# One program block for the state space stage of a hybrid trunk layer: set-up, four turns and end part written out, with one run of gate columns

## The reference

```python
def ssm_mixer(u, lam_re, lam_im, log_dt, b_re, b_im, c_re, c_im, d_skip, glu_w, glu_b):
    ...
    _, _, xr, xi = lax.associative_scan(combine, (a_r, a_i, bur, bui), axis=1)
    y = (jnp.einsum('bsgp,gcp->bsgc', xr, c_re.astype(f32))
         - jnp.einsum('bsgp,gcp->bsgc', xi, c_im.astype(f32))).reshape(B, S, SSM_WIDTH)
    y = jax.nn.gelu(y + d_skip.astype(f32) * uf)
    y = y * jax.nn.sigmoid(y @ glu_w.astype(f32) + glu_b.astype(f32))
    return y.astype(u.dtype)
...
        ga, gb, gc = jnp.split(jax.nn.sigmoid(h @ gate_w[l] + gate_b[l]), N_BRANCHES, axis=-1)
```

## Time and profile before

| | us |
|---|---|
| median of 3 runs | 3227.89 (3226.14 to 3228.81) |
| the profiled execution | 3229.56 |
| its span, first to last instruction | 3227.3 |
| TensorE busy in it | 2858.8 (89%) |
| VectorE busy | 1984.2 (61%) |
| ScalarE busy | 1472.7 (46%) |
| GpSimd busy | 390.5 (12%) |

### The profile page before, as it was taken

How to read it: one execution, slowest core, us unless ns; L and a number is a source line. 1 busy time by engine, 2 the same in 40 slices (tenths; PEclk the granted TensorE clock), 3 DMA queues, 4 the chain that set the end, 5 groups by cost and what they waited for, 6 DMA issues and landing times. The chain is left out here.

```text
span 3227.3 us, 41692 instructions
## 1 busy us (share of the span) xinstructions
PE 2858.8 (89%) x13494; PEld 2213.1 (69%) x13495; DVE 1984.2 (61%) x3048; ACT 1472.7 (46%) x2363; POOL 390.5 (12%) x296
## 2 busy tenths in 40 slices
PE   4999998999999987889995987994899999999994
PEld 3767666676767765777774776883677777777772
DVE  6657994545454554544353654225788888888883
ACT  4315553545555552222233332121566666666662
POOL 3101220000000001110010000110122122222211
PEclk9999998999999998888897998996999999999997
DMA  6374324141313136211117996542889997866864
GB/s 234 103 244 169 96 92 144 33 134 37 121 44 115 40 115 203 66 43 45 42 62 270 291 298 215 178 159 111 310 282 298 348 355 248 279 213 215 282 191 137
DMA packets 289051, 553.55 MB, mean 172 GB/s; under 512 B 30745, under 2 KB 97561, under 8 KB 284834
## 3 DMA queue, kind: packets, MB, share of 16 engines
q1 hardware_dynamic: 271010, 500.45, 44.8%
q0 software_dynamic: 14112, 51.39, 6.7%
q10 hardware_dynamic: 3808, 0.14, 0.1%
HBM read 417.16 MB, written 143.15 MB: 174 GB/s over the span
## 5 line engine op out<-in xcount | busy, mean ns | idle before, releaser
L2512 DVE TENSOR_TENSOR moe_w_lo<-moe_W,moe_w_hi 128x1024 fp32r<-128x1024 f32 x392 | 471.3, 1221 | 84.4 <-ACT moe_w_hi L2448 80.1
L2448 ACT CAST moe_w_hi<-moe_W 128x1024 fp32r (+1 forms) x392 | 409.2, 1050 | 145.8 <-PE moe_h1b L2379 77.6
L1573 PE MATMUL project_bank<-h_lo,w_hi 128*128 128x512 f32 x512 | 204.6, 400 | 0.0
L515 DVE TENSOR_SCALAR_CACHE_REDUCE att_S<-att_bank 128x512 f32<-128x512 f32 x192 | 125.0, 689 | 120.3 <-PE att_bank L303 120.3
L336 PE MATMUL att_bank<-h_hi,w_hi 128*128 128x512 f32 x384 | 171.1, 445 | 14.1 <-PEq L137 10.8
L2404 PE MATMUL moe_yb<-moe_W,moe_hT 128*128 x384 | 172.8, 593 | 0.0
L2377 PE MATMUL moe_h1b<-moe_w_hi,moe_xT_hi 128*128 128x512 f32 x384 | 157.1, 409 | 3.8 <-DVE moe_xT_lo L2523 3.8
L421 ACT ACTIVATE att_S<-att_S,att_nm 128x128 f32<-128x128 f32 (+15 forms) x128 | 154.1, 1206 | 0.0
L337 PE MATMUL att_bank<-h_lo,w_hi 128*128 128x512 f32 x384 | 153.0, 398 | 0.0
L2378 PE MATMUL moe_h1b<-moe_w_lo,moe_xT_hi 128*128 128x512 f32 x384 | 152.6, 397 | 0.0
L338 PE MATMUL att_bank<-h_hi,w_lo 128*128 128x512 f32 x384 | 152.6, 397 | 0.0
(11 more groups left out here) (460 smaller groups left out, 6980.3 us busy)
## 6 DMA issues: line engine op xcount, KB each, us to landing
moe_W<-in_moe_w SPq DMA_DIRECT2D x96, 2048.0 KB, 10.6
w_raw<-in_gate_w SPq DMA_DIRECT2D x48, 512.0 KB, 3.7
out_sg<-gateT SPq DMA_DIRECT2D x32, 768.0 KB, 8.3
gateT<-att_gates SPq DMA_DIRECT2D x48, 256.0 KB, 2.4
gateT<-gate_out SPq DMA_DIRECT2D x48, 256.0 KB, 2.4
early<-in_ada_w SPq DMA_DIRECT2D x8, 1024.0 KB, 9.6
project_spare<-in_x SPq DMA_DIRECT2D x16, 512.0 KB, 6.8
w_raw<-in_w_in SPq DMA_DIRECT2D x16, 512.0 KB, 4.2
```

Source lines behind the costliest of these rows:

```text
L1573: pe.matmul(bank[n % 4][:], w_hi[b][:, k, :], low[:, k, at512(tb)], start=False, stop=False)
L2448: nc.scalar.copy(w_hi[:, slot(p, first), :], raw(at, p)).then_inc(q["w13_high"], 1)
L2512: nc.vector.tensor_tensor(w_lo[:, own, :], raw(at, p), w_hi[:, own, :].bitcast(F32), ALU.subtract).then_inc(q["w1_low" if p < 4 else "w3_l ...
```

## The change

Set-up, turns and end part become one block. The loop is written out in the Python source (`for tn in range(TURNS)`), so each turn has its own instructions and its indices are constants. The five `s.end()` between the parts are gone (the one at the stage's end stays); semaphores run on through the turns, their values counted up with `tn`. One `GateFill` of 21 chunks takes the place of the three kinds of run, so that `higher` of a part's first chunk stands behind the last `out` of the part before. The bias is read from `gate_bias` at a constant column, and GpSimd's copy of it (`take_bias`) goes. The copies to `ucp` and `c1` for a turn are made in the turn ahead of it, behind its last RJ. VectorE builds E of a turn before it waits for the y products of the turn ahead (`y_summed`), and `apt` and M2 behind that wait. A semaphore `set_up` tells ScalarE and VectorE that C2 is there.

The diff, cut to its core:

```diff
-            "gb": gate_bias,
-            "gbt": sb("gate_gbt", [P, 8], ctx=ctx)}
+            "gb": gate_bias}
...
-    def take_bias(self, pool):
-        self.nc.gpsimd.tensor_copy(self.tiles["gbt"][:, :self.count], self.tiles["gb"][:, bass.ds(self.c0, self.count)]).then_inc(self.biased, 1)
...
-        if u == 0:
-            act.wait_ge(self.biased, 1)
-                                  bias=self.tiles["gbt"][:, u // 2:u // 2 + 1]).then_inc(self.placed, 1)
+                                  bias=self.tiles["gb"][:, self.c0 + u // 2:self.c0 + u // 2 + 1]).then_inc(self.placed, 1)
...
-        fill_set = GateFill(nc, g, s, tiles, h_hi, h_lo, 3, 4, 0)
+        fill = GateFill(nc, g, s, tiles, h_hi, h_lo, 3, 21, 0, last=True)
...
+                for tn in range(TURNS):
+                    for u in range(8 + 6 * tn, 14 + 6 * tn):
+                        fill.store(sp, u)
...
+                for j in range(20):
+                    fill.lower(pool, j)
...
+                pe.wait_ge(q["placed"], 8)
                 for n in range(KD, 8 * KD):
-                    fill_set.group(pe, n)
+                    fill.group(pe, n)
+
+                for tn in range(TURNS):
+                    ident = const(g, "ident")
+                    base = (8 + 6 * tn) * KD
+                    pe.wait_ge(q["u_copied"], 2 * tn + 1)
+                    for b in range(2):
+                        for gi in (2 * b, 2 * b + 1):
+                            for f in range(2):
+                                at = (gi % 2) * SC + f * P
+                                mm = pe.transpose(bank[b][:, at:at + P], ucp[:, f, gi, :], ident)
+                        mm.then_inc(q["u_turned"], 1)
+                    for done in range(8):
+                        fill.group(pe, base + done)
...
+                    pe.wait_ge(q["u_copied"], 2 * tn + 2)
...
+                    pe.wait_ge(q["m_placed"], tn + 1)
+                    if tn:
+                        pe.wait_ge(q["y_placed"], 2 * tn)
+                    for b in range(2):
...
+                for tn in range(TURNS):
+                    mine = slice(tn * GU, (tn + 1) * GU)
+                    if tn == 0:
+                        act.wait_ge(q["placed"], 8)
+                        nc.scalar.copy(ucp[:], UY[:, :, mine, :]).then_inc(q["u_copied"], 1)
+                        act.wait_ge(q["set_up"], 1)
+                        nc.scalar.copy(c1[:], C1[:, mine, :]).then_inc(q["u_copied"], 1)
+                    for b in range(2):
+                        act.wait_ge(q["u_turned"], 2 * tn + b + 1)
+                        nc.scalar.copy(U[:, 2 * b:2 * b + 2, :].rearrange("p g n -> p (g n)"), bank[b][:]).then_inc(q["u_placed"], 1)
+                    fill.out(act, 8 + 6 * tn)
+                    act.wait_ge(q["m2_ready"], tn + 1)
+                    for lv in range(LEVELS):
+                        if lv in (2, 4, 6):
+                            fill.out(act, 8 + 6 * tn + lv // 2)
+                        for gi in range(GU):
+                            if LEVELS * tn + lv >= 2:
+                                act.wait_ge(q["r_ready"], GU * (LEVELS * tn + lv - 2) + gi + 1)
+                            nc.scalar.activation(RJ[:, lv % 2, gi, :], const(g, "swap"), ACT.Copy,
+                                                 scale=apt[:, 1, lv, gi:gi + 1]).then_inc(q["rj_ready"], 1)
+                    if tn + 1 < TURNS:
+                        after = slice((tn + 1) * GU, (tn + 2) * GU)
+                        act.wait_ge(q["u_turned"], 2 * tn + 2)
+                        nc.scalar.copy(ucp[:], UY[:, :, after, :]).then_inc(q["u_copied"], 1)
+                        act.wait_ge(q["k_summed"], tn + 1)
+                        nc.scalar.copy(c1[:], C1[:, after, :]).then_inc(q["u_copied"], 1)
+                    fill.out(act, 12 + 6 * tn)
+                    fill.out(act, 13 + 6 * tn)
+                    for f in range(2):
+                        act.wait_ge(q["y_summed"], 2 * tn + f + 1)
+                        nc.scalar.copy(UY[:, f, mine, :], bank[4 + f][:].rearrange("p (g n) -> p g n", g=GU)).then_inc(q["y_placed"], 1)
+
+                act.wait_ge(q["y_placed"], 2 * TURNS)
+                for n, (hc, f, i0) in enumerate(units):
+                    if n >= 2:
+                        act.wait_ge(q["y_turned"], n - 1)
+                    for i in range(4):
+                        ins = nc.scalar.copy(ycp[:, n % 2, i, :].rearrange("p (g c) -> p g c", c=16),
+                                             UY[:, f, hc * 8:(hc + 1) * 8, (i0 + i) * 16:(i0 + i + 1) * 16])
+                    ins.then_inc(q["u_copied"], 1)
+                    if n == 6:
+                        fill.out(act, 32)
...
-                link(ts(C2[:].rearrange("p g c -> p (g c)"), bank[5][:, 256:512], -1.0, None, ALU.mult))
-        s.end()
-
-        with nc.Fori(0, GROUPS // GU) as turn:
-            fill = GateFill(nc, g, fill_set, tiles, h_hi, h_lo, turn * 3 + 7, 3, 1)
...
+                ts(C2[:].rearrange("p g c -> p (g c)"), bank[5][:, 256:512], -1.0, None, ALU.mult).then_inc(q["set_up"], 1)
+                dve.wait_ge(q["set_up"], 1)
+
+                for tn in range(TURNS):
+                    mine = slice(tn * GU, (tn + 1) * GU)
...
+                    if tn:
+                        dve.wait_ge(q["m2_ready"], tn)
+                        dve.wait_ge(q["k_summed"], tn)
                     by_power(E[:, :, 0:SL, :], Et[:], prev, B1, B2, q["e_ready"])
+                    if tn:
+                        dve.wait_ge(q["rj_ready"], GU * LEVELS * tn)
+                        dve.wait_ge(q["r_ready"], GU * LEVELS * tn)
+                        dve.wait_ge(q["y_summed"], 2 * tn)
                     link(nc.vector.tensor_copy(apt[:], ap[:, :, :, mine]))
...
-                    nc.scalar.copy(ucp[:], UY[:, :, mine, :]).then_inc(q["u_copied"], 1)
-                    nc.scalar.copy(c1[:], C1[:, mine, :]).then_inc(q["u_copied"], 1)
-                    for b in range(2):
-                        act.wait_ge(q["u_turned"], b + 1)
-                        nc.scalar.copy(U[:, 2 * b:2 * b + 2, :].rearrange("p g n -> p (g n)"), bank[b][:]).then_inc(q["u_placed"], 1)
-                    fill.higher(act, 0)
-                    fill.out(act, 0)
-                    act.wait_ge(q["m2_ready"], 1)
-                    for lv in range(LEVELS):
-                        if lv in (2, 4, 6):
-                            fill.out(act, lv // 2)
-                        for gi in range(GU):
-                            if lv >= 2:
-                                act.wait_ge(q["r_ready"], GU * (lv - 2) + gi + 1)
...
-            s.end()
-
-        G2 = 2 * math.sqrt(2 / math.pi)
-        fill_end = GateFill(nc, g, fill_set, tiles, h_hi, h_lo, 19, 5, 1, last=True)
-        with nc.Block() as block:
-            units = [(hc, f, i0) for hc in range(2) for f in range(2) for i0 in (0, 4)]
```

More of the change, by code:

```diff
@@ new lines, in _ @@
+                for n, (hc, f, i0) in enumerate(units):
+                    if n >= 4:
+                        pe.wait_ge(q["skipped"], n - 3)
+                    pe.wait_ge(q["u_copied"], 2 * TURNS + n + 1)
+                    for i in range(4):
+                        mm = pe.transpose(bank[n % 4][:, i * P:(i + 1) * P], ycp[:, n % 2, i, :], const(g, "ident"))
+                    mm.then_inc(q["y_turned"], 1)
+                    fill.group(pe, 32 * KD + 2 * n)
+                    fill.group(pe, 32 * KD + 2 * n + 1)
@@ new lines, in _ @@
+                for n in range(34 * KD, 38 * KD):
+                    fill.group(pe, n)
+                pe.wait_ge(q["y_placed"], 2 * TURNS)
+                for n in range(8):
+                    c, tb = n % 2, n // 2
+                    pe.wait_ge(q["gelued"], 4 + tb + 1)
+                    if n >= 2:
+                        pe.wait_ge(q["glued"], n - 1)
+                    for k in range(2):
+                        mm = pe.matmul(bank[4 + n % 2][:], glu[:, k, c * P:(c + 1) * P], ycT[:, k, tb * 512:(tb + 1) * 512],
+                                       start=k == 0, stop=k == 1)
+                    mm.then_inc(q["opened"], 1)
+                    for done in range(38 * KD + 4 * n, 38 * KD + 4 * n + 4):
+                        fill.group(pe, done)
@@ new lines, in _, with high @@
+                fill.out(act, 33)
+                for n in range(8):
+                    c, tb = n // 4, n % 4
+                    b = uc[:, c, tb * 512:(tb + 1) * 512]
+                    act.wait_ge(q["squared"], n + 1)
+                    nc.scalar.activation(b, b, ACT.Sigmoid, scale=G2).then_inc(q["gated"], 1)
+                    if n in (2, 5):
+                        fill.out(act, 34 + n // 3)
+                fill.out(act, 36)
+                fill.out(act, 37)
+                def high(n):
+                    c, tb = n % 2, n // 2
+                    act.wait_ge(q["ready"], n + 1)
+                    if n >= 2:
```

(14 more changed lines are left out.)

276 lines of the change are left out of this document (79 added, 197 removed).

## The result

| | before | after |
|---|---|---|
| median of 4 runs each | 3227.11 us (3226.14 to 3228.81) | 3181.46 us (3179.59 to 3188.54) |
| profiled execution, its span | 3229.56, 3227.3 | 3188.54, 3186.7 |
| ratio | | 0.9863, 95% interval 0.9849 to 0.9876 |

The changed kernel is faster by 45.65 us; 36.1 were forecast.

The account below looks back on a forecast made before the run. The stage was taken as bound by TensorE's instruction stream plus five idle holes. Waits of 26.05 us and clock of 10.1 summed to 36.1, taking 3227.89 to 3191.8 us; the range was 3184 to 3200.

Parts of the forecast that it names:

- The first hole: TensorE's idle time at the head of the first turn falls from 8.50 to 2.65 us, saving 5.85 us.
- The three holes between turns: TensorE's waits at the heads of turns two to four go entirely, saving 16.9 us.
- wait for `u_copied`: Sign of being wrong: TensorE waits for the U copies each turn; that case had 3218.7 us, chance 0.02.
- The end part: TensorE starts the end part at 1638.44 instead of 1641.74, saving 3.30 us and leaving a hole of 1.69.
- The clock behind the holes: Five low-clock stretches after TensorE's idle holes, 26.30 us busy, go; at 0.44 lost this returns 11.6 us.
- The fall behind the hole of 2.65 us: At the first turn's head the clock still drops after the remaining idle time, taking 1.5 us off the saving.
- The narrow products: Within each turn L1137 brings the clock down for 10.14 us; the likeliest case left this unchanged.
- Low stretches other than ten us: Sign of being wrong: low-clock stretches at L1137 inside the turns with a length other than ten us.
- The rival with shorter stretches: Low-clock stretches at L1137 get shorter, 1.5 us per turn, 6.0 over four: 3185.8 us, chance 0.12.
- What costs nothing: GpSimd's w_lo may delay VectorE's M2 by 2.1 us, 5.8 at most against ScalarE's ten: cost 0 each turn.
- Slower by code: Fetching four written-out turns stalls TensorE, 1.5 us a block; 30 more blocks give 3236.8 us, chance 0.02.
- The rival with longer stretches: Low-clock stretches at L1137 get longer, 1.5 us per turn, 6.0 over four: 3197.8 us, chance 0.13.

Follow-up runs that it names:

- a1: The changed kernel run once more, nothing altered, for a second trace: 3182.33 us, ratio 0.9871.
- e_heads: The changed kernel, but each turn's copies to `ucp` and `c1` made at its own head instead of the turn ahead: 3192.82 us, ratio 0.9895.
- e_kmix: The changed kernel with the twelve gate groups ahead of the narrow products spread between them (six stay ahead in the first turn): 3170.45 us, ratio 0.9823.
- a_mix6: The changed kernel with six gate groups ahead of the narrow products and six between them in every turn: 3177.52 us, ratio 0.9848.
- b1: The kernel before run once more, nothing altered, for a second trace: 3225.98 us, ratio 0.9996.
- best: The changed kernel with gate groups spread between the narrow products and the first `ucp` and `ycp` copies made earlier, in set-up and last turn: 3173.3 us, ratio 0.9829.
- e_unroll: The kernel before with only its loop written out in the source, block ends, clears and barriers kept: 3219.01 us, ratio 0.9976.
- e_split: The changed kernel with the rounding of each part's first gate weights put back behind the U copies: 3192.88 us, ratio 0.9892.
- e_sems: The kernel before with 40 more unused semaphores, so each block end clears 87 instead of 47: 3241.39 us, ratio 1.0049.
- e_ahead: The changed kernel with the first `ucp` copy moved into set-up and the first two `ycp` units' copies into the last turn: 3187.06 us, ratio 0.9881.
- b_mix6: The kernel before with six gate groups ahead of the narrow products and six between them in every turn: 3218.26 us, ratio 0.9969.

## Why the prediction missed, step by step

**The first hole, 5.85 us: right.** The trace has 2.66 for 2.65, and the set-up is 5.71 us shorter.

**The three holes between turns, 16.9: right.** No wait is left, and no wait for `u_copied`.

**The end part, 3.30: right.** 1.60 us are left for 1.69. The hole lies ahead of the part's first product, so its gain is in the last turn's distance; the part itself is 1.4 us shorter (74.40 to 73.03), which is the clock behind the hole.

**The clock behind the holes, 11.6: right, and a little more.** All low stretches behind holes are gone, in every version without `s.end()`. At 0.48 they are worth 12.6, on 26.3 us of low clock.

**The fall behind the hole of 2.65 us, -1.5: wrong.** The rows disagreed for gaps of 2.40, and I took the dearer side. In none of the five traces with this hole (after, `a1`, `e_heads`, `e_kmix`, `a_mix6`) did the clock fall there; in `a1`, the hole and what follows it up to the narrow products:

```profile
1331.14:1333.80 2.66, 0.00 (x2) 0.01 (x1) 2.52 (x5) 2.62 (x4) 0.93 (x1) 1.00 0.26 102
1333.80:1343.50 9.70, 9.70 (x48) 8.06 (x49) 5.18 (x6) 4.12 (x12) 1.76 (x1) 1.00 0.27 82
```

A gap of 2.70 us elsewhere, which ends at 243.91 in `b1`, was followed by a fall at once. The length of the gap does not settle it.

**The narrow products, L1137 left at 10.14 us in the likeliest case: wrong, and the step that cost the range.** The sum had no term for them; "the work in front of them stays" was the argument. But in `a1` the fall came 4.8 to 5.4 us behind their start instead of 3.6. Four times 10.24 became 6.83, 6.83, 6.83 and 10.24 in `a1`: 10.2 us x 0.48 = 4.9, half of the 10.3 us that the forecast lacked; without them the time would be 3186.4 us, inside the range. Low stretches other than ten us were one of the prediction's own signs of being wrong. Why the fall comes where it does stays open. The rival with shorter stretches had the mechanism, one step of 1.5 us per turn; but it stood alone, as if the first hole's 1.5 and it excluded each other. Together with it the forecast is 3185.8 - 1.5 = 3184.3, just inside the range and still 2.8 us above what was measured.

The sum for `a1`: 36.1 + 4.9 (narrow products) + 1.5 (no fall at the first hole) + 1.0 (price 0.48) + 0.8 (shorter way to the merge, chance) = 44.3; its stage is 44.5 shorter. The medians are 45.65 apart; the last 1.2 us have no place in the stage, and of the 10.3 us another 0.8 are the median of before, which a fourth run moved from 3227.89 to 3227.11. The trace of after, with four low stretches of 13.65, has only 32.6 in the stage, and gained the other 8.0 us of its 40.6 outside it, where the change takes away no more than one small GpSimd copy: projection 6.3 shorter, merge 4.4 shorter, attention 3.7 longer, the rest small. The projection took 471.7 us there and 478.0 in before, but 473.1 in `a1` and 481.1 in `best`, with the same instructions. So the last two microseconds of an agreement in one trace prove little.

**What costs nothing: right.** GpSimd's w_lo (1332.88, 2.69 us) held VectorE's L1208 for 2.74 us instead of 0.69, as in the earlier trace rows, 2.05 us. It fell on E at the first head, which TensorE needed far later, and not on M2 as the prediction had it; in the other turns it was over (1397.21 + 2.36 = 1399.57 in the second) before M2's instructions began at 1399.66. M2 was ready 4.6 us after the head in the first turn (1337.70 + 0.69) and 2.9 in the second, before RJ, which start 7.3 us after the head (1406.16 - 1398.88). Before, these were 3.7 and ten; the room is smaller than the prediction had it, and the cost is still 0. The Trainium skill (SBUF — State Buffer, "Who interferes with whom") says that a VectorE instruction with two SBUF inputs and a GpSimd one that reads SBUF contend; the 2.05 us at L1208 agree.

**Slower by code: did not occur.** Seven blocks more, where the rival asked for 24; the waits of TensorE inside the turns name its own sequencer nowhere, and `e_unroll` with the same 78 is faster than before.

The rival with longer stretches, 3197.8, was not idle either: the trace of after has just its longer stretches, 13.65 for 10.24, and two of eight executions of after and `a1` were at 3188.5 and 3192.2. That the median fell on the side of the shorter ones is luck as far as the prediction goes. A kernel with two forms asks for a range that spans both.

## What to carry to other kernels

Price a barrier with its semaphore clears in full (5.0 to 5.7 us here, and half as much again through the clock that falls behind it, 12.6 us over five), and pull the next stretch's first copies in front of it or remove it. Where a run of small products brings the clock down, mix large ones between them before going for the last microseconds of waits: here that was worth 11 us, while taking away 4.3 us of waits gained nothing that could be measured, as the low stretches grew longer with it. When the timing ahead of such a run moves, let the forecast's range carry every length of the low stretch that the traces know, up and down, at each of its repetitions.

## What the runs showed of the hardware

**A busy TensorE is not a TensorE at full clock.** In the narrow products TensorE is busy without a gap by the traces, and yet the clock falls 2.4 to 5.5 us behind their start, wherever they stand without gate groups between them. With the groups spread between them (`e_kmix`, `best`) it fell in none of the eight turns. The length of the low stretch goes with how early the fall comes: at 2.4 to 3.0 us it was 13.65 (after, `e_split` and `e_sems` four times each, `e_ahead` three, `e_heads` once), at 3.5 to 4.8 us 10.24 (before and `b1` four times each, `e_heads` three, `e_unroll` two, `e_ahead` and `a1` once), at 5.0 to 5.5 us 6.83 (`a1` three times, `e_unroll` two). In `a1` the fall comes 0.18 us earlier from turn to turn (5.37, 5.19, 5.00, 4.83), and with the last of these steps the stretch is 3.4 us longer. What sets where it falls was not found; the rows only say that the length is known once the fall is, and that only for this order: with six groups between the products it was 17.07 us for a fall at 3.3 (`b_mix6`).

**One semaphore clear costs some 62 ns.** That is by the 40 more of `e_sems`. The 47 of this stage take 2.66 us on SyncE at the end of each turn, about half of each hole of 5.0 to 5.7.

**The same instructions in the same kernel's other stages vary** by up to 9 us between traces (the projection, 471.7 to 481.1 us), in the main with the low stretches they catch: TensorE was busy at the lower level for 5.8 us of it in after, 17.0 in before and 19.5 in `best`.
